# The weight ring at the top of SBUF instead of between the activations and the constants

## What is computed

```
for l in range(2):
    x = layer_norm(ALPHA*x + 0.5*swiglu(x, ffn1_w1[l], ffn1_w3[l], ffn1_w2[l]))
    y = hybrid_mixer(x, ...)        # four attention mixers of 4 heads of 64; x @ w_in, ..., @ w_out
    x = layer_norm(ALPHA*x + y)
    x = layer_norm(ALPHA*x + 0.5*swiglu(x, ffn2_w1[l], ffn2_w3[l], ffn2_w2[l]))
proj = rmsnorm(x) @ w_in_2
y_ssm = mamba2_mixer(...) @ w_out_ssm_2      # chunked state-space scan, width 2048
y_lru = rglru_mixer(...) @ w_out_lru_2       # gated linear recurrence, width 1280
h = x + (g_ssm*y_ssm + g_lru*y_lru) @ w_out_2
h = h + (silu(hn @ w_gate) * (hn @ w_up)) @ w_ffn_out_2     # hn = rmsnorm(h)
out = rmsnorm(h)
```

## Time and profile before

| | |
|---|---|
| median of 3 runs | 3969.5 us (3957.92 to 3971.23) |
| the profiled execution, its span | 3995.3 us |
| instructions | 44,743 |
| PE busy | 3604.5 us, 90% |
| PEld busy | 2815.3 us, 70% |
| DVE busy | 1782.0 us, 45% |
| ACT busy | 1451.4 us, 36% |
| POOL busy | 48.8 us, 1% |
| mean granted TensorE clock | 0.939 |
| DMA | 276.78 MB, mean 69 GB/s, 21% of 16 engines' span |

### The profile page before, as it was taken

One profiled execution on the slowest core, in us unless ns is written; L12 is line 12 of the kernel. 1 busy time (PEld: TensorE's weight loads), 2 busy tenths in 40 slices (PEclk: granted clock), 3 DMA queues, 4 the chain that ended last, 5 costly groups with the idle time before them and its releaser, 6 DMA issues. The chain is left out here.

```text
span 3995.3 us, 44743 instructions
## 1 busy us (share of the span) xinstructions
PE 3604.5 (90%) x16162; PEld 2815.3 (70%) x16200; DVE 1782.0 (45%) x2970; ACT 1451.4 (36%) x2379; POOL 48.8 (1%) x44
## 2 busy tenths in 40 slices
PE   7999989988999899988998899958888897889998
PEld 6877657766888688866677687836676675667876
DVE  3333458435332433344864433265655446534333
ACT  4322425353332433242545332244544335323322
POOL 0000020000000000001000000000000000000000
PEclk9999998688999899999898999979999998999999
DMA  3332210002332123221001233211121122222331
GB/s 134 95 106 72 99 44 1 1 27 69 96 105 88 64 94 101 88 88 60 1 1 37 70 99 102 82 33 44 53 64 59 58 79 66 73 70 90 94 104 59
DMA packets 73728, 276.78 MB, mean 69 GB/s; under 512 B 10368, under 2 KB 11904, under 8 KB 72832
## 3 DMA queue, kind: packets, MB, share of 16 engines
q1 hardware_dynamic: 73600, 275.12, 21.1%
HBM read 272.99 MB, written 2.10 MB: 69 GB/s over the span
## 5 line engine op out<-in xcount | busy, mean ns | idle before, releaser
L341 PE MATMUL ps<-xh,whi 128*128 128x512 f32 x2880 | 1151.1, 400 | 166.4 <-DVE xl L482 70.2
L342 PE MATMUL ps<-xl,whi 128*128 128x512 f32 x2880 | 1135.2, 394 | 0.0
L343 PE MATMUL ps<-xh,wlo 128*128 128x512 f32 x2880 | 1134.0, 394 | 0.0
L313 DVE TENSOR_TENSOR wlo<-raw,whi 128x1024 fp32r<-128x1024 f32 (+2 forms) x464 | 602.4, 1298 | 1075.4 <-ACT whi L309 1075.4
L341 PEld LDWEIGHTS ps<-xh,whi 128*128 128x128 f32 x2880 | 549.4, 191 | 311.7 <-issue 142.1
L309 ACT ACTIVATE whi<-raw 128x1024 fp32r<-128x1024 f32 (+2 forms) x464 | 514.7, 1110 | 509.4 <-PE ps L343 501.4
L343 PEld LDWEIGHTS ps<-xh,wlo 128*128 128x128 f32 x2880 | 549.6, 191 | 117.7
L342 PEld LDWEIGHTS ps<-xl,whi 128*128 128x128 f32 x2880 | 550.9, 191 | 112.6 <-issue 2.4
L341 PE MATMUL ps<-ffn_hh,whi 128*128 128x512 f32 x880 | 350.6, 398 | 12.6 <-DVEq L607 12.6
L343 PE MATMUL ps<-ffn_hh,wlo 128*128 128x512 f32 x880 | 349.8, 397 | 0.0
L342 PE MATMUL ps<-ffn_hl,whi 128*128 128x512 f32 x880 | 349.7, 397 | 0.0
(11 more groups left out here) (327 smaller groups left out, 3940.0 us busy)
## 6 DMA issues: line engine op xcount, KB each, us to landing
raw<-in_ffn_up SPq DMA_DIRECT2D x216, 512.0 KB, 3.5
raw<-in_ffn_down SPq DMA_DIRECT2D x80, 704.0 KB, 4.0
raw<-in_mix_in SPq DMA_DIRECT2D x40, 512.0 KB, 3.5
raw<-in_ssm_in SPq DMA_DIRECT2D x40, 512.0 KB, 3.6
raw<-in_lru_in SPq DMA_DIRECT2D x20, 512.0 KB, 3.5
raw<-in_mix_out SPq DMA_DIRECT2D x16, 512.0 KB, 3.2
raw<-in_ssm_out SPq DMA_DIRECT2D x12, 512.0 KB, 3.7
raw<-in_lru_out SPq DMA_DIRECT2D x8, 640.0 KB, 3.9
```

The costliest lines, as they stand in the source:

```text
L313: dve.tensor_tensor(self.core.wlo[:, u % HALF, 0:width], self.core.raw[:, u, 0:width], self.core.whi[:, u % HALF, 0:width].bitcast(F32), A ...
L341: pe.matmul(out, c.whi[:, h, w], xh[:, k0 + k], start=first and k == 0, stop=False)
L342: pe.matmul(out, c.whi[:, h, w], xl[:, k0 + k], start=False, stop=False)
L343: mm = pe.matmul(out, c.wlo[:, h, w], xh[:, k0 + k], start=False, stop=last and k == nk - 1)
```

## The change

The ring goes behind the work area; the constants and the work area move down by the ring's 45,056 bytes. Nothing else is different: the program of each engine has the same instructions in the same order with the same waits (only the line numbers are 3 higher).

```diff
-A_X, A_XH, A_XL, A_RAW, A_WHI, A_WLO = 0, 16 * KB, 32 * KB, 48 * KB, 48 * KB + RAW * SLOT * 4, 48 * KB + (RAW + HALF) * SLOT * 4
-A_CONST = A_RAW + (RAW + 2 * HALF) * SLOT * 4
+WORK_BYTES = 100 * KB
+A_X, A_XH, A_XL, A_CONST = 0, 16 * KB, 32 * KB, 48 * KB
...
 A_KB = A_PAR + 128 * 4
 A_WORK = A_KB + N_BF16 * P * 2
+A_RAW = A_WORK + WORK_BYTES
+A_WHI = A_RAW + RAW * SLOT * 4
+A_WLO = A_WHI + HALF * SLOT * 4
```

## The result

| | median us | lowest to highest | runs |
|---|---|---|---|
| before | 3968.09 | 3957.92 to 3971.23 | 4 |
| changed | 4016.46 | 4008.05 to 4024.25 | 4 |

The recorded ratio is 1.0097, with a 95% interval of 1.0055 to 1.014 (the quotient of the two medians is 1.0122). The forecast was 3969 us, "same"; the time lies above the range's end of 4006.

The account below looks back on a forecast made before the run. PE was taken to bound the kernel, with ring-weight matmuls 68% of the span. Every term was put at 0, summing to 0 of the profiled 3995.3 us, carried over to the median of 3969.5 us; range 3952 to 4006.

Parts of the forecast that it names:

- What bounds the kernel: Whole kernel: PE, busy 90%, sets the end; 11,904 ring-weight matmuls take 2722 us, 68% of the span.
- The reading by what is left after division by 64: Ring matmuls: moving operands starting on a multiple of 64 take 226.9 ns, those 32 bytes past it 233.5.
- the second rival: Ring matmuls: differing operand starts slow the stream, so xh and ffn_hh swap paces; +35.5 us, 4005 us; chance 0.07.
- the ring as stationary operand: Weight loads from 32 past a multiple of 64 stay covered; taken as 0, upper end +78.6 us.
- The first rival: Ring matmuls: off-boundary weight loads disturb the stream; 173 and 168 matmuls in 40 us; chance 0.10, small form included.
- splits: ScalarE and VectorE splits of ring weights: 1050 and 1225 ns for 1024 numbers as before; cost 0, 8 us if uncovered.
- loads: Ring loads of 4096-byte rows: still 3.5 us to land; cost 0 to 2.2 us, taken as 0.
- the exposed start: Kernel start: 7.9 us for the first two ring tiles and 5.8 for the constants, expected unchanged.
- PE's wait for `wlo`: PE: a wait grown past its 38.1 us would show the prediction wrong.
- height: Work area and constants 44 KB down: taken as 0, within 21.5 us either way; as faster rival -21.5 us, chance 0.05.
- the load as covered: Ring matmuls: the weight load's 0.115 us is about half of the 0.227 us a matmul lasts, so hidden.

Follow-up runs that it names:

- e10: TensorE alone, no network: start differences 0, 32, 64, 128 bytes across types, moving and weight columns; fp32r 512 columns, 128 weight columns: 226.6, 233.3, 229.0, 232.7 ns.
- e5: The sweep: TensorE alone, no network, 24 fp32r matmuls for each pair of start addresses; 226.6 to 226.9 ns a matmul at difference 0, 233.3 at 32.
- e6: Kernel before with the ring 32 bytes higher in place, x, xh, xl and work area unmoved; 4002.8 us at equal clock, ratio 1.0049.
- e8: Changed kernel with the bf16 constants, work area and ring at the top 32 bytes lower; 3946.8 us at equal clock, ratio 0.9942.
- e7: Kernel before with the bf16 constants and work area 32 bytes lower; 3945.0 us at equal clock against 3969.0, ratio 0.9942.
- e9: Kernel before with wlo alone 32 bytes higher (fp32 constants 64 up); 4053.36 us at clock 0.937, none at equal clock.
- e2: Changed kernel with the ring at the top 32 bytes higher, on a multiple of 64 again; 4024.1 us at equal clock, ratio 1.0100.
- e4: Changed kernel with x, xh, xl 32 bytes higher and the rest 64 higher; 4003.8 us at equal clock, ratio 1.0050.

## Why the prediction was wrong

**What bounds the kernel** was right: PE, and 68% of the span in the ring's matmuls. That an address costs time there, 178 against 173, was right too.

**The reading by what is left after division by 64 was wrong.** It came from one coincidence: the slow operands all lay 32 past a multiple of 64. The sweep has xh's stream at remainder 160 as fast as at 128, if the weights go along (227.3 ns against 226.7), and slow at remainders on a multiple of 64, if they do not (233.6 ns at a difference of 128, 233.3 at 192). In the earlier trace rows the stretches with 172 or 173 matmuls also had another difference from the ring than those with 178; that reading, the second rival, fitted the rows as well.

**The step that failed** is the one on the ring as stationary operand, "I take 0: the two direct comparisons of loads are equal". Lines 1618 and 1285 compare loads under fp32 matmuls of 8 and 64 columns. e10 finds no step for fp32 at any of its four differences, with 512 columns (429.2 ns a record), and none for fp32r at 256 (119.7 ns at difference 0, 117.7 to 118.8 at the others); 8 and 64 columns of fp32 were not tried, but nothing says that they would show it. The term put at 0 was +34 us. Lines 1028 and 1265, which I held against the second rival, are single records of 64 rows in groups of three whose first takes 0.34 us; their operands are at difference 0 and took 0.23 and 0.24 us, where a steady row takes 0.227. They are no steady row, and e5 shows what that means: the first five distances of the row at 212.45, also at difference 0, are 229 to 236 ns. So 0.23 and 0.24 us do not speak for the slow pace.

**The second rival was the truth, with its number.** It had 173 and 178 matmuls, +35.5 us and 4005 us; the runs at equal clock show +34.4 and, in e6, +33.8, and 8640 x 6.4 - 3264 x 6.6 = +34. It got a chance of 0.07 where the evidence against it was void. Its rule, equal starts, was right in kind; its period, 64 bytes as I wrote it down, was not: it is 256. That its number came out owes something to luck: the change makes differences of 0 and 224 bytes out of 32 and 0, and 224 costs as much as 32, where 64 costs a third (233.2, 233.3 and 228.9 ns against 226.7). The first rival has a small form in its chance of 0.10; no run shows that form or a size for it. What the changed kernel showed in its place is 233.3 ns for the ring's matmuls with xh and 226.7 for those with ffn_hh.

**The range** ended at 4006, and the median was 4016.46 because two of four runs had, by their clocks and times, the long stretch at granted clock 0.50 and, by their times, none of before's four had; the other two, at 0.942 and 0.943, lie 2 and 3 us above 4006 as well. I noted that the profiled execution lay 25.8 us above the median and let it pass as a constant. It was a second mode of the clock, visible as a 6 in the PEclk row.

**The rest** came out as forecast: splits 1050 and 1225 ns, loads 3.5 us, the exposed start 7.8 and 5.8 us, PE's wait for `wlo` not grown (35.6 us), height without effect (e8 within 1.8 us of e7). I took the load as covered, 0.115 us of 0.227. The sweep's row with the weights alone moved by 32 bytes took 233.4 ns against 226.7 even so: for fp32r at 512 columns the start of the weights alone changes the pace. For fp32 and bf16 the four differences show no such effect (429.2 ns a record, 215.8 a matmul).

## What to carry to other kernels

Where fp32r matmuls of 512 columns run back to back, start the moving operands and the stationary ones at the same remainder of 256 bytes: it was 226.7 ns a matmul against 233.3, and one constant changed by 32 bytes gave 0.6% here. When two stretches differ in pace, list every way in which their addresses differ, the differences between operands too, and sweep them with TensorE alone before choosing one: 111 rows of pairs took 0.8 ms in one run. Compare a program of this kind at equal mean granted clock, since one stretch at granted clock 0.50 can outweigh the effect sought: before took 3992 to 3997 us at 0.938 or 0.939 against 3968 at 0.946, and e7's gain is 24.0 us.

## What the runs showed of the hardware that was not expected

- The pace of fp32r matmuls, 128x128 by 512 columns, goes by the difference of the two start addresses modulo 256: 226.7 ns at 0, 228.9 at 64, 233.2 to 234.3 at the other multiples of 32 (e5). Moving either operand by whole 4096 bytes, by up to 163,840, leaves it at 226.6 to 227.2.
- At 24 matmuls a row of 512 columns, bf16 took 215.8 ns a matmul and fp32 858.3 (two records of 429.2) at each of the four differences (e10).
- One of the two weight buffers off by 32 bytes brings the three matmuls of a block to a mean of 233.2 or 233.3 ns, whichever buffer it is (e9).
- Of 58 later runs of before, 30 had a mean clock of 0.941 or less, and 18 of 36 of the other kernels whose up-projection runs at 227 ns. Of the kernels with the up-projection at 233 ns (the changed one in both jobs, e2, e4, e6), 6 of 43 had. These are counts over unlike kernels in several jobs. By them the slower pace seems to spare the program most of the long stretches at granted clock 0.50, which gives back part of the loss in a mean over all runs. Why a mixer falls to 0.50 in some executions is open.
